# Delta-rule heads: the norms of q and k moved behind the products

## The reference, cut to what matters

```python
q_g = l2_normalize(q_g)            # x * rsqrt(sum(x * x) + EPS), over the 128 of a head
k_g = l2_normalize(k_g)
g = -exp(a_log) * softplus(gdn_a + dt_bias)
beta = sigmoid(gdn_b)
# in chunks of tokens (64 here, 128 in the kernel):
m   = where(strict, beta_i * (k_i . k_j) * decay_ij, 0)
sol = triangular_solve(I + m, [v * beta, k * beta * exp(g)])
intra = where(lower_incl, (q_i . k_j) * decay_ij, 0)        # q carries 128 ** -0.5
state = state * exp(g_last) + (k * exp(g_last - g))^T v_new
o   = (q * exp(g)) state + intra v_new
o_g = rms_norm(o_g, gdn_norm_w) * silu(gdn_gate)
```

## Time and profile before

| | |
|---|---|
| time, median of 3 runs | 1124.35 us (1124.12 to 1124.72) |
| span of the profiled execution | 1125.6 us, one core; no time of its own stands beside it |
| TensorE busy (page) | 1108.7 us, 99% |
| VectorE, ScalarE, GpSimd busy | 548.7, 577.9, 438.1 us |
| TensorE's idle time by its waits, all | 11.4 us, of it 2.9 us in the four delta heads' L573 |
| the four delta heads run | from about 73 to 376 us |

### The profile page before, as it was taken

One profiled execution on the slowest core, in us unless ns is written; L12 is line 12 of the kernel. 1 busy time (PEld: TensorE's weight loads), 2 busy tenths in 40 slices (PEclk: granted clock), 3 DMA queues, 4 the chain that ended last, 5 costly groups with the idle time before them and its releaser, 6 DMA issues.

```text
span 1125.6 us, 15293 instructions
## 1 busy us (share of the span) xinstructions
PE 1108.7 (99%) x5869; PEld 898.2 (80%) x5869; DVE 548.7 (49%) x1167; ACT 577.9 (51%) x1066; POOL 438.1 (39%) x236
## 2 busy tenths in 40 slices
PE   8999999999999999999999999999999999999997
PEld 7777877878778888889777777779888888888886
DVE  3638869779575314134345445735211114544444
ACT  5546766767767752254455556645322234333333
POOL 4144234342351444545122332324544445544441
PEclk9899999999999999999999999999999999999999
DMA  9222122221231323633322222212333333322212
GB/s 258 67 76 56 39 75 57 57 68 46 57 94 38 87 89 106 212 88 78 95 58 57 77 75 95 75 57 76 112 94 94 96 107 116 113 94 94 94 56 75
DMA packets 140378, 97.25 MB, mean 86 GB/s; under 512 B 8865, under 2 KB 124938, under 8 KB 140306
## 3 DMA queue, kind: packets, MB, share of 16 engines
q1 hardware_dynamic: 136704, 91.09, 27.6%
q10 hardware_dynamic: 3602, 5.18, 1.4%
HBM read 93.35 MB, written 2.90 MB: 86 GB/s over the span
## 4 chain that ended last, share of the span: by engine, by line
PE 94%; DVE 3%; ACT 1%; issue 1%; POOL 1%; DMA 1%; SPq 0%; DVEq 0%; ACTq 0%
PE bank L433 31%; PE bank L1176 14%; PE bank L1158 14%; PE bank L462 6%; PE bank L828 4%; PE bank L837 4%; PE bank L853 4%; PE bank L1189 2%; PE bank L998 1%; PE bank L651 1%; PE bank L669 1%; PE bank L594 1%; PE bank L982 1%; PE bank L989 1%; PE bank L582 1%; PE bank L963 1%
## 5 line engine op out<-in xcount | busy, mean ns | idle before, releaser
L2461 POOL TENSOR_TENSOR ring<-raw_ring,ring 128x1024 fp32r<-128x1024 f32 x160 | 391.7, 2452 | 593.0 <-ACT ring L1202 593.0
L433 PE MATMUL bank<-hT,ring 128*128 128x512 f32 x1536 | 404.0, 407 | 1.3 <-POOL ring L2461 1.3
L433 PEld LDWEIGHTS bank<-hT,ring 128*128 128x128 f32 x1536 | 279.3, 189 | 67.7 <-issue 13.5
L1202 ACT CAST ring<-raw_ring 128x1024 fp32r<-128x1024 f32 x160 | 167.4, 1048 | 112.1 <-PE bank L1176 90.3
L1176 PE MATMUL bank<-ring,ring_u 128*128 128x512 f32 x672 | 154.0, 391 | 0.0
L1158 PE MATMUL bank<-hT,ring 128*128 128x512 f32 x672 | 152.5, 389 | 0.0
L1176 PEld LDWEIGHTS bank<-ring,ring_u 128*128 128x128 f32 x672 | 126.2, 188 | 27.6
L1158 PEld LDWEIGHTS bank<-hT,ring 128*128 128x128 f32 x672 | 126.1, 188 | 26.1
L2436 DVE TENSOR_TENSOR ring_u<-u,ring_u 128x1024 fp32r<-128x1024 f32 x32 | 81.1, 2540 | 75.0 <-ACT ring_u L1790 75.0
L2441 DVE TENSOR_TENSOR u<-u 128x512 f32<-128x512 f32 x32 | 22.9, 715 | 139.2 <-ACT u L1797 139.2
L1797 ACT ACTIVATE u<-bank 128x512 f32<-128x512 f32 x32 | 19.1, 598 | 115.3 <-PE bank L1158 108.4
(11 more groups left out here) (298 smaller groups left out, 1521.4 us busy)
## 6 DMA issues: line engine op xcount, KB each, us to landing
raw_ring<-in_w_in SPq DMA_DIRECT2D x144, 256.0 KB, 3.3
raw_ring<-in_w_up SPq DMA_DIRECT2D x64, 256.0 KB, 3.1
raw_ring<-in_w_down SPq DMA_DIRECT2D x64, 256.0 KB, 2.8
raw_ring<-in_w_out SPq DMA_DIRECT2D x32, 256.0 KB, 2.8
x<-in_x SPq DMA_DIRECT2D x4, 512.0 KB, 5.6
raw_ring<-in_w_branch_sb SPq DMA_DIRECT2D x8, 256.0 KB, 2.9
raw_ring<-in_w_branch_gdn SPq DMA_DIRECT2D x8, 256.0 KB, 3.2
x<-in_x ACTq DMA_DIRECT2D x4, 512.0 KB, 5.9
```

Source lines behind the costliest of these rows:

```text
L433: p = pe.matmul(bank, m.slab_k8(n % 4)[:, a, k, :], m.hT[:, b, k, :], start=term == 0, stop=term == 23)
L1202: act.copy(m.ring[:, q, 0, :], m.raw_ring[:, q, :]).then_inc(s.slab_hi[q], 1)
L2461: pool.tensor_tensor(m.ring[:, q, 1, :], m.raw_ring[:, q, :], m.ring[:, q, 0, :].bitcast(F32), ALU.subtract).then_inc(s.slab_lo[q], 1)
```

## The change

q and k stay unnormalised.

- k: TensorE transposes kT to token rows where the sum of q's squares stood (`delta_k_rows`, new, 4 transposes into bank 6). ScalarE squares the rows with an accumulated sum for each of the four chunks, then a logarithm and two exponentials on 128x4 values (`delta_k_norm`, new body). VectorE's `delta_keys` (new, ahead of `stick_soft(i, 0)`) multiplies the gates of beta by the square of the reciprocal norm or by the reciprocal norm, on 128x4 values, and writes kd and bk from bank 6. `delta_rows` and both 512-wide multiplications of `delta_normed` go; its product for v stays (`delta_values`). GpSimd's `delta_masks` uses the new gate.
- q: its square, times a constant, is kept in a new buffer `q_sq` (ScalarE, now in the middle of the head). At the head's end VectorE adds it to the square of the output before the product with ones, so that EPS counts as in the reference.
- `delta_q_sum` and `delta_k_sum` go.

The core of the diff:

```diff
-    def delta_q_sum(i):
-        pe.wait_ge(s.qk_sq, 2 * i + 1)
+    def delta_k_rows(i):
+        pe.wait_ge(s.k_dve, 2 * i + 2)
         if i:
             pe.wait_ge(s.state, 7 * i - 1)
         else:
             pe.wait_ge(s.small_dve, 13)
-        pe.matmul(banks[6], mat["ones"], MT if i else tmp, start=True, stop=True).then_inc(s.delta_ps, 1)
-
-    def delta_k_sum(i):
-        pe.wait_ge(s.qk_sq, 2 * i + 2)
-        if i:
-            pe.wait_ge(s.o_act, 4 * (i - 1) + 2)
-        else:
-            pe.wait_ge(s.small_act, 11)
-        pe.matmul(banks[5], mat["ones"], XT, start=True, stop=True).then_inc(s.delta_ps, 1)
+        for c in range(4):
+            p = pe.transpose(chunk(banks[6], c), chunk(kT, c), ident)
+        p.then_inc(s.delta_ps, 1)
 
...
-        pe.wait_ge(s.qk_norm, 3 * i + 2)
+        if i:
+            pe.wait_ge(s.o_act, 4 * (i - 1) + 2)
+        else:
+            pe.wait_ge(s.small_act, 11)
         for c in range(4):
             p = pe.matmul(chunk(banks[5], c), chunk(kT, c), chunk(kT, c), start=True, stop=True)
         p.then_inc(s.delta_ps, 1)
-        pe.wait_ge(s.rnorm, 4 * i + 1)
+        pe.wait_ge(s.q_dve, 2 * i + 2)
+        pe.wait_ge(s.bk_kd, 2 * (i + 1))
         for c in range(4):
             p = pe.matmul(chunk(banks[6], c), chunk(kT, c), chunk(qT, c), start=True, stop=True)
-        p.then_inc(s.delta_ps, 1)
-        pe.wait_ge(s.qk_norm, 3 * i + 3)
-        for c in range(4):
-            p = pe.transpose(chunk(banks[7], c), chunk(kT, c), ident)
         p.then_inc(s.delta_ps, 1)
...
     def delta_o_sum(i):
-        pe.wait_ge(s.o_act, 4 * i + 1)
+        pe.wait_ge(s.o_dve, 4 * i + 2)
         pe.matmul(banks[5], mat["ones"], tmp, start=True, stop=True).then_inc(s.o_sum, 1)
...
         tiles.to(4)
-        delta_q_sum(i)
+        delta_k_rows(i)
         tiles.to(14)
...
-        delta_k_sum(i)
...
     tiles.to(10)
-    delta_q_sum(i)
+    delta_k_rows(i)
     tiles.to(22)
     delta_decay(i)
-    tiles.to(27)
-    delta_k_sum(i)
...
     def delta_q_square(i):
+        if i:
+            act.wait_ge(s.o_dve, 4 * (i - 1) + 2)
         act.wait_ge(s.q_dve, 2 * i + 2)
-        act.activation(q_tile(i), qT, ACT.Square).then_inc(s.qk_sq, 1)
-
-    def delta_k_square(i):
-        act.wait_ge(s.k_dve, 2 * i + 2)
-        act.activation(XT, kT, ACT.Square).then_inc(s.qk_sq, 1)
+        act.activation(m.q_sq, qT, ACT.Square, scale=P * EPS ** 0.5).then_inc(s.q_sq, 1)
+
+    def delta_k_norm(i):
+        ks = m.k_stat
+        act.wait_ge(s.delta_ps, 6 * i + 1)
+        for c in range(4):
+            p = act.activation(chunk(XT, c), chunk(banks[6], c), ACT.Square, accum_out=ks[:, 0, c:c + 1])
+        p.then_inc(s.k_norm, 1)
+        act.wait_ge(s.k_norm, 4 * i + 1)
+        act.activation(ks[:, 0, :], ks[:, 0, :], ACT.Ln, bias=m.eps_c).then_inc(s.k_norm, 1)
+        act.wait_ge(s.k_norm, 4 * i + 2)
+        act.activation(ks[:, 1, :], ks[:, 0, :], ACT.Exp, scale=-0.5).then_inc(s.k_norm, 1)
+        act.activation(ks[:, 2, :], ks[:, 0, :], ACT.Exp, scale=-1.0).then_inc(s.k_norm, 1)
...
-    def delta_q_norm(i):
-        act.wait_ge(s.delta_ps, 8 * i + 1)
-        act.activation(q_tile(i), banks[6], ACT.Ln, bias=m.eps_c).then_inc(s.rnorm, 1)
-        act.wait_ge(s.rnorm, 4 * i + 1)
-        act.activation(q_tile(i), q_tile(i), ACT.Exp, scale=-0.5).then_inc(s.rnorm, 1)
-
-    def delta_k_norm(i):
-        act.wait_ge(s.delta_ps, 8 * i + 3)
-        act.activation(XT, banks[5], ACT.Ln, bias=m.eps_c).then_inc(s.rnorm, 1)
-        act.wait_ge(s.rnorm, 4 * i + 3)
-        act.activation(XT, XT, ACT.Exp, scale=-0.5).then_inc(s.rnorm, 1)
...
+        act.wait_ge(s.o_dve, 4 * i + 1)
...
-        act.activation(tmp, banks[5], ACT.Ln, bias=m.eps_c, scale=1.0 / P).then_inc(s.o_act, 1)
+        act.activation(tmp, banks[5], ACT.Ln, bias=m.eps_q, scale=1.0 / P).then_inc(s.o_act, 1)
...
-        delta_q_norm(i)
+        delta_k_norm(i)
...
-        delta_k_norm(i)
+        delta_q_square(i)
...
-        delta_q_square(i + 1)
         stick_out(i)
         delta_out(i)
         tile_a(g + 6)
         delta_out_high(i)
-        delta_k_square(i + 1)
...
-    delta_q_norm(i)
+    delta_k_norm(i)
     merge_tile(0)
-    delta_k_norm(i)
     delta_decay(i)
+    delta_q_square(i)
     log_of_sigmoid(gate, m.rawg, s.g_sig, 4 * i)
...
-    def delta_normed(i):
-        dve.wait_ge(s.rnorm, 4 * i + 2)
-        dve.scalar_tensor_tensor(qT, qT, P ** -0.5, MT if i else tmp, ALU.mult, ALU.mult).then_inc(s.qk_norm, 1)
-        times(kT, kT, XT, s.rnorm, 4 * i + 4, s.qk_norm)
-        dve.wait_ge(s.delta_ps, 8 * i + 4)
-        dve.tensor_tensor(v4(bv), v4(banks[7]), along(m.gates[:, i, 1, :]), ALU.mult).then_inc(s.qk_norm, 1)
+    def delta_keys(i):
+        ks = m.k_stat
+        if i == 0:
+            dve.wait_ge(s.small_dve, 20)
+        dve.wait_ge(s.k_norm, 4 * (i + 1))
+        dve.tensor_tensor(ks[:, 4:6, :], m.gates[:, i, 1:3, :], ks[:, 2:3, :].broadcast_to([P, 2, 4]), ALU.mult).then_inc(s.k_gate, 1)
+        dve.tensor_tensor(ks[:, 3, :], m.gates[:, i, 1, :], ks[:, 1, :], ALU.mult).then_inc(s.k_gate, 1)
+        dve.tensor_tensor(v4(kd), v4(banks[6]), along(m.gates[:, i, 3, :]), ALU.mult).then_inc(s.bk_kd, 1)
+        dve.wait_ge(s.k_gate, 3 * i + 1)
+        dve.tensor_tensor(v4(bk), v4(banks[6]), along(ks[:, 5, :]), ALU.mult).then_inc(s.bk_kd, 1)
+
+    def delta_values(i):
+        dve.wait_ge(s.delta_ps, 6 * i + 3)
+        dve.wait_ge(s.k_gate, 3 * i + 2)
+        dve.tensor_tensor(v4(bv), v4(banks[7]), along(m.k_stat[:, 3, :]), ALU.mult).then_inc(s.k_gate, 1)
...
-    def delta_rows(i):
-        dve.wait_ge(s.delta_ps, 8 * i + 7)
-        dve.tensor_tensor(v4(bk), v4(banks[7]), along(m.gates[:, i, 2, :]), ALU.mult).then_inc(s.bk_kd, 1)
-        dve.tensor_tensor(v4(kd), v4(banks[7]), along(m.gates[:, i, 3, :]), ALU.mult).then_inc(s.bk_kd, 1)
...
         dve.tensor_copy(X, banks[7]).then_inc(s.o_dve, 1)
+        dve.wait_ge(s.o_act, 4 * i + 1)
+        dve.wait_ge(s.q_sq, i + 1)
+        dve.tensor_tensor(tmp, tmp, m.q_sq, ALU.add).then_inc(s.o_dve, 1)
         dve.wait_ge(s.o_act, 4 * i + 3)
...
         stick_qk(i)
+        delta_keys(i)
         stick_soft(i, 0)
         delta_decay(i)
-        delta_normed(i)
+        delta_values(i)
         stick_soft(i, 1)
         delta_gram(i)
         delta_zero(i, 4)
         delta_substitute(i, 0, 15)
-        delta_rows(i)
         delta_blocks(i)
...
+    delta_keys(i)
     delta_decay(i)
     merge_least(0)
     delta_zero(i, 4)
-    delta_normed(i)
+    delta_values(i)
     delta_gram(i)
     merge_least(1)
     least(gate, m.rawg, s.g_sig, 4 * i + 3, s.g_dve)
-    delta_rows(i)
     delta_zero(i, 5)
     stick_qk(i)
     merge_least(2)
...
         pool.wait_ge(s.decay_exp, 3 * i + 2)
-        pool.tensor_tensor(v4(Cb), v4(Cb), along(m.gates[:, i, 1, :]), ALU.mult).then_inc(s.decay_in, 1)
+        pool.wait_ge(s.k_gate, 3 * i + 1)
+        pool.tensor_tensor(v4(Cb), v4(Cb), along(m.k_stat[:, 4, :]), ALU.mult).then_inc(s.decay_in, 1)
```

More of the change, by code:

```diff
@@ L135, in __init__ @@
         self.eps_c, self.one_c, self.zero_c, self.lam_c = little("eps_c", 1), little("one_c", 1), little("zero_c", 1), little("lam_c", 1)
+        self.eps_q = little("eps_q", 1)
         self.half_c, self.far = little("half_c", 4), little("far", 4)
@@ L183, in __init__ @@
         self.diag, self.diag_inv = (take(name, [P, P]) for name in ("diag", "diag_inv"))
+        self.q_sq = take("q_sq", [P, T])
         self.diag_invT = self.banks[6][:, 0:P]
@@ L2492, in residual @@
         norm_rstd(r + 1, 3, 4)
-    pool.wait_ge(s.memsets, 3)
+    pool.wait_ge(s.memsets, 4)
     norm_rstd(0, 0, 0)
```

31 lines of the change are left out of this document (16 added, 15 removed).

## The result

| | before | after |
|---|---|---|
| time, median | 1124.23 us (1124.04 to 1124.72, 4 runs) | 1131.99 us (1129.9 to 1134.53, 4 runs) |
| ratio | | 1.0064, 95% interval 1.005 to 1.0078 |
| span and clock of the profiled execution | 1125.6 us, 0.996 | 1129.7 us, 0.997 (its time: 1131.0 us) |

What follows compares the result with a forecast made beforehand. The prediction took TensorE, busy 1108.7 of 1125.6 us, as the bound. Its terms, -6.9 + 1.9 + 2.8 + 7.6 = +5.4 us, carried to the median of 1124.35, gave 1129.8 us, range 1122.8 to 1133.5.

Steps and rivals of the forecast that it cites:

- Eight products with ones: On TensorE, eight products with ones dropped, each 0.86 us and gained in full: -6.9 us.
- the transposes moved: kT's transposes on TensorE, free behind the wait for L1955, cost 0.47 us a head at the new place: +1.9 us.
- The addition: At the head's end, VectorE's add of q's square delays the output's product with ones: 3 x 0.73 + 0.6 = +2.8 us.
- The wait for kT: At kT's transposes in heads 1 to 3, TensorE waits since GpSimd's second slab holds VectorE ahead of kT's product: +7.6 us.
- E + 4.0: When kT is ready, counted from E, the end of GpSimd's L2461 (first slab); E + 1.8 before.
- The point from which it decides: GpSimd's second slab doesn't get in ahead of kT's product if its cast on ScalarE ends after E + 0.5.
- The chain behind the transposes: ScalarE's `delta_k_norm`, about 2.5 us, and VectorE's `delta_keys`, about 1.6 us, are covered: 0, up to 2 us if too long.
- The work taken from `delta_rows`: VectorE's work removed from `delta_rows` and `delta_normed` falls where nobody waits for VectorE: 0 gain.
- rival 3: TensorE's clock falls behind the two waits of 2.9 us, 3.4 us lost each: 1136.6 us, chance 0.08.
- Rivals 1 and 2: First: second slab doesn't get in between, 1123.7 us, chance 0.17. Second: TensorE's operands are early after all, 1119.3, chance 0.08.
- rival 1: GpSimd's second slab doesn't get in ahead of kT's product, kT at E + 1.8: sum -0.6, 1123.7 us, chance 0.17.

Runs made afterwards that it cites:

- e2: Changed kernel with VectorE's last products of kT and v moved to right behind the new add; median 1121.03 us, 1121.0 at full clock, ratio 0.9962 to the kernel before.
- e1: Changed kernel with ScalarE's last slab cast in each loop waiting for kT's product again; median 1123.16 us, 1121.9 at full clock, ratio 0.9981 to the kernel before.
- e3: Changed kernel with a one-column copy in place of the addition of q's square; median 1128.15 us, 1125.5 at full clock, ratio 1.0028 to the kernel before.
- second group of runs: Runs on another chip, among them the changed kernel again, unaltered: median 1132.46 us, ratio 1.0052, beside the kernel before at 1125.81.

## Why the prediction was right, point by point

**Eight products with ones, and the transposes moved: -6.9 + 1.9 = -5.0.** In the profile after, TensorE is at L545 in head 0 at 72.16 and at the first gram product at 86.62; before at 73.68 and 89.40:

```profile
72.16 0.60 PE L545 MATMUL bank<-consts,g 128*128 128x128 f32 x4
...
86.62 1.05 PE L561 MATMUL bank<-g 128*128 128x128 f32 x8
...
89.73 0.66 PE L570 MATMUL bank<-consts,g 128*128 128x128 f32 x4 [1.16 <-DVE g L1955]
90.22 0.60 PE L655 MATMUL bank<-consts,s 128*128 128x128 f32 x4
```

14.46 instead of 15.72 us: 1.26 less, for 2 x 0.86 - 0.47 = 1.25. From the gram product to L655 it is 3.60 us, as before (89.40 to 93.00), with four transposes fewer in it: the 0.47 us went into the wait. Right, both terms.

**The addition: +2.8.** Measured by taking it out: 2.6. From the second L598 (L595 after) to the product with ones the profiles have 0.71, 0.70, 0.73 and, in head 3, 0.57 us more than before: 2.7, head by head as forecast. Right.

**The wait for kT: +7.6.** From the product with ones to the transposes of kT it is 10.27, 10.25 and 10.30 us in the three heads (138.28 to 148.55 in the first), where the kernel before took 7.37, 7.38 and 8.73: 2.90 + 2.87 + 1.57 = 7.3. The prediction had 2.9, 2.9 and 1.5 by products and took 7.6, a mean with the reading by loads; the products had it. By e2, which takes the wait away, it is 7.1. The mechanism, its three places and E + 4.0 are right. The point from which it decides (a cast that ends after E + 0.5) was not probed closely: in the changed kernel the cast ends 0.7 us ahead of E and the slab gets in, in e1 it ends 2.9 us behind E and does not.

**The chain behind the transposes: 0.** It was covered: there is no wait at L655. It was also shorter than the 2.5 us of the prediction, since the accumulator's reads lie beside the next square. ScalarE's first square and its last exponential:

```profile
149.24 0.28 ACT L1310 ACTIVATE g<-bank 128x128 f32<-128x128 f32 x1 [3.96 <-PE bank L545]
...
150.86 0.19 ACT L1316 ACTIVATE stat<-stat 128x4 f32<-128x4 f32 x1
```

1.8 us from first to last.

**The work taken from `delta_rows`: 0, and this step failed.** The prediction put it that this falls "in stretches in which nobody waits for VectorE: 0, with no gain since TensorE has no wait there to shorten". From the first gram product to the second level's L598 the kernel before took 26.81 us in head 0 (89.40 to 116.21), and after takes 26.41 (86.62 to 113.03). The prediction had read from the list of waits that everywhere else the small products are ready when TensorE comes to them. That list does not hold these 0.4 us, because it goes by the modelled ends of products; the loads do. VectorE's two products of `delta_rows` stood directly ahead of the operations on which these loads wait, 1.2 us of them. Before, then after:

```profile
103.33 0.68 DVE L2000 TENSOR_TENSOR g<-bank,gates 128x512 f32<-128x512 f32 x1
103.93 0.68 DVE L2001 TENSOR_TENSOR g<-bank,gates 128x512 f32<-128x512 f32 x1
105.33 0.67 DVE L1993 TENSOR_TENSOR g<-diag_inv,consts 128x512 f32<-128x512 f32 x1
...
106.11 0.97 PEld L582 LDWEIGHTS bank<-g,g 128*128 128x128 f32 x8 [0.26 <-issue]
...
115.27 0.97 PEld L594 LDWEIGHTS bank<-g,g 128*128 128x128 f32 x8 [0.49 <-ACT g L1376]
```

```profile
101.50 0.67 DVE L1993 TENSOR_TENSOR g<-diag_inv,consts 128x512 f32<-128x512 f32 x1
...
103.13 1.08 PEld L579 LDWEIGHTS bank<-g,g 128*128 128x128 f32 x8
...
112.00 1.05 PEld L591 LDWEIGHTS bank<-g,g 128*128 128x128 f32 x8
```

Before, L1993 ended at 106.00 and the load followed at 106.11; after, it ended at 102.17, 1 us ahead of the load. Heads 1 and 2 gain 0.40 and 0.39 us in the same stretch. Head 3 gains 0.02 (37.02 before, 37.00 after): its `delta_rows` stood at 317.13, ahead of the whole substitution, and its load at L582 waited for nobody before either. Together this is **-1.2 us**. That `delta_rows` is the cause is read from the timelines and from this difference between the heads; it was not changed alone.

With the sizes measured from start to start the sum is -5.0 + 2.7 + 7.3 - 1.2 = +3.8, against 3.8 to 3.9 at full clock. From head 0's first step to head 3's product with ones the profiles have 301.08 us before and 306.52 after, +5.4, of it 1.6 to 1.8 of the clock behind head 1 (from L545 to the first gram product head 1 takes 16.03 us, heads 0 and 2 take 14.46 and 14.47): +3.6 to 3.9. The same terms give the experiments. Without the wait for kT it is -5.0 + 2.7 - 1.2 = -3.5 against 1124.3 for the kernel before: 1120.8, and e2 has 1121.0. With e1's 1.1 us of waiting it is 1121.9, and e1 has 1121.9. Without the addition it is 1125.4, and e3 has 1125.5.

**The clock, which the prediction had as rival 3 with a chance of 0.08.** It came on top of the forecast and not in place of it: the forecast's waits came, and of the 7.8 us of the median nearly 4 are the clock. (In the second group of runs it is 6.7 us between the medians, of which less than 3 are the clock, as the kernel before had slower runs there too.) The prediction asked for two falls with a loss of 3.4 us each; the profiles have one, of 1.7 to 1.8. What lowers the clock in the slower runs, down to 0.993, is not known, since no profile of them was kept. That the time, 1131.99, lies so near to 1129.8 is in part luck, two errors of opposite sign: +5.4 forecast for the order of work where +3.8 was measured, and nothing for the clock where it took nearly 4.

**Rivals 1 and 2** are out by the profile after: L2034 took 2.84 us, so the slab did get in, and TensorE waits at both operands, L625 and L545. e1 makes rival 1 come true: its time is 1121.9 at full clock and not the 1123.7 of the prediction, again mostly for the 1.2 us of `delta_rows`.
